# Gate matrix of an expert layer: one-hot products for 128 tokens, scattered adding transfers for the other 128

## The chip, the cores and the metric

One core of a Trainium2 chip runs the whole program: TensorE (PE in the profile; its weight loads are PEld), VectorE (DVE), ScalarE (ACT), GpSimd (POOL), SyncE (SP) and 16 DMA engines. The metric is the device time of one execution in microseconds, as the median of the runs. Less is better.

## What is computed

The reference is a transformer-like block followed by a second block, on 256 tokens of width 2048, all in float32. The part that matters here is the expert layer (PEER) of the second block: every token picks 16 experts in each of 8 heads, out of 128 x 128 experts, and gives each a gate.

```python
cand_i = (i1[..., :, None] * PEER_KEYS + i2[..., None, :]).reshape(t, PEER_HEADS, -1)
top_s, pos = lax.top_k(cand_s, PEER_TOPK)
expert = jnp.take_along_axis(cand_i, pos, axis=-1).reshape(t, -1)
gate = jax.nn.softmax(top_s.astype(jnp.float32), axis=-1).astype(x.dtype).reshape(t, -1)
...
z = jnp.einsum('cd,ced->ce', xc, u[ec])
act = jax.nn.gelu(z, approximate=False) * gc
return jnp.einsum('ce,ced->cd', act, v[ec])
```

The kernel computes it densely. For all 16384 experts it forms `z = x @ u.T`, takes the gelu, multiplies by a gate matrix G that holds the summed gate of each (expert, token) pair and is zero where the token did not pick the expert, and multiplies by `v`. G is 128 blocks of experts by 256 tokens, with 128 experts of each block on the partitions: 16.8 MB, which is the whole of the SBUF tensor `big`.

## The kernel before

**The stream.** All weights, `u` and `v` among them, arrive as 902 units of 512 KB (128 partitions x 1024 float32), two units to a pair, through four buffers `raw` that SP loads (L598). Each unit is split into a high part in float32r (`split_hi`, ACT, L474) and a low rest (`split_lo`, DVE, L483), and PE multiplies with both. A load is issued when the low half of the unit four earlier is made; ACT and DVE split units up to four ahead of PE (`w_hi`, `w_lo` have four slots each; both wait on `unit_done`). A unit is 8 matmuls of 512 columns on the high part (L540) and 8 of 256 columns on the low part (L547) in `halves_out`.

**The stages of the expert layer.** One pair of `u` gives one block of 128 experts. The 128 blocks go through three loops, then `v` is multiplied.

- `u_decode` (with `wqu`): 32 blocks while the router's picks are made.
- `u_gates`: 64 blocks, 32 turns of two pairs. Between the high and the low products of each pair, PE makes the gates of four tokens (L2558, `four_tokens`): one matmul of a one-hot of the second index (`hot`, 128x128, made by POOL at L686) with a one-hot of the first index that carries the gate's high and low half (`weighted`, 128x256, made by DVE at L2023). ACT copies the low half of the result from PSUM to G (L1160), DVE adds the high half (L2017). 64 pairs x 4 tokens = 256 tokens.
- `u_late`: 32 blocks, whose gelu is multiplied by G at once. The blocks before them could not be, since G was not there: ACT stores each to a DRAM tensor `z_kept` (128 KB a block), and `late_turn` and the first half of the `v` loop read them back into `cst` and multiply.

So the 96 early blocks make the way over DRAM, and the 32 late ones don't. The order on each engine is written out by hand; PE, ACT and DVE meet through counting semaphores. Before the gates loop the three lists of picks (first index, second index, gate; 256 tokens x 128 slots each) are transposed by PE (L2548), six matmuls of 128x128.

The kernel is built with `dynamic_dma_scratch_size=1024`, the bytes per partition that are reserved for the descriptors of POOL's transfers; before the change POOL issues none. POOL's queue in this part: staging copies of the attention (L647), sums of the router, then the 256 compares at L686, then the gain of the output at the end (L692).

Of the kernel before, what the change touches and what calls it, by code (L numbers as in the profile page):

```python
# [65 lines left out]
SLOT_N = PH * PK  # L66

# [3 lines left out]
         ("wqu", 4 * PH), ("u_decode", 2 * PH), ("u_gates", S // 4), ("u_late", NB // 4), ("v", NB)]  # L71
EARLY = 3 * NB // 4
LATE = NB - EARLY
# [11 lines left out]
for _name, _count in [("conv", 4 * CONV_J), ("rnn", 2 * KT), ("heads", 2 * H2), ("u_decode", 2 * PH), ("u_gates", S // 4),  # L85
                      ("u_late", LATE)]:
    HALVED[_name] = _n
    _n += _count
# [5 lines left out]
for _name, _count in [("ident", P), ("iota", P), ("band", TT * 2 * P), ("causal", TT * S), ("cos", TT * HALF),  # L94
                      ("sin", TT * HALF)]:
    CONST[_name] = (_n, _n + _count)
    _n += _count
# [37 lines left out]
def build(nc, stream, x, p_t, rows, consts, params, rg_w, ukv, keys_t, out):  # L135
    ctx = ExitStack()
    with ctx:
# [24 lines left out]
        with nc.sbuf_tensor("expert_act", [P, 2, 2, S], F32R) as expert_act:  # L162
            pass
        weighted = sb("weighted", [P, 4, 2, P], F32R)
# [10 lines left out]
        x_kept = nc.dram_tensor("x_kept", (P, TT * D), F32, kind="Internal").ap()  # L175
        z_kept = nc.dram_tensor("z_kept", (EARLY, P, S), F32, kind="Internal").ap()

# [98 lines left out]
        first_index = slot_t[:, 0, :]  # L276
        second_index = par[:, 0:S]
        gate_hi = slot_t[:, 1, :]
        gate_lo = slot_t[:, 2, :]
        GATE_BANKS = [[banks[0], banks[1]], [banks[4], banks[5]]]  # L280
# [31 lines left out]
        idx8 = stat[:, 8:16]  # L312
# [123 lines left out]
        hot_turn = sem("hot_turn")  # L436
        hot1 = sem("hot1")
        hot2 = sem("hot2")
# [148 lines left out]
        primed = [y_made, z_saved, early_ready, scored, rg_done, logits_made, hot2, hot_used, conv_b_used,  # L587
# [45 lines left out]
        def _(pool):  # L633
# [6 lines left out]
            pool.sem_inc(pool_summed, 4)  # L640

            for t in range(TT):
# [34 lines left out]
            pool.wait_ge(slots_kept, 3)  # L677

            with pool.Fori(0, S // 8) as i:
                pool.wait_ge(hot2, i * 8 + 1)  # L680
                pool.tensor_copy(idx8, second_index[:, bass.ds(i * 8, 8)]).then_inc(g_step, 1)
                pool.wait_ge(g_step, i + 1)
                for s in range(8):
                    pool.wait_ge(hot_used[s % 4], i * 2 + s // 4 + 1)
                    pool.sem_inc(hot_turn, 1)
                    pool.tensor_scalar(hot[:, s % 4, :], iota, idx8[:, s:s + 1], None, ALU.is_equal)\  # L686
                        .then_inc(hot2, 1)
# [9 lines left out]
        def _(act):  # L697
# [439 lines left out]
            for a in range(3):  # L1137
                act.wait_ge(picks_turned, 2 * a + 2)
                act.activation([first_index, second_index, gate_lo][a], banks[4 + a][:, 0:S], ACT.Copy).then_inc(slots_kept, 1)
# [13 lines left out]
            def gates_turn(i, first=False):  # L1153
                for n in range(2):
# [3 lines left out]
                    for half in range(2):  # L1158
                        act.wait_ge(hot_used[2 * half + 1], i * 2 + n + 2)
                        act.activation(G[:, :, bass.ds(i * 8 + (4 * n + 2 * half), 2)],  # L1160
                                       GATE_BANKS[n][half].rearrange("p (t a b) -> p a b t", t=2, a=2)[:, 1, :, :],
                                       ACT.Copy).then_inc(gate_low, 1)
# [6 lines left out]
            with act.Fori(1, S // 8) as i:  # L1169
                gates_turn(i)  # L1170
            save_gelu(S // 8 - 1, 1)
# [92 lines left out]
        def _(dve):  # L1264
# [737 lines left out]
            for a in range(3):  # L2002
                ins = dve.tensor_copy(PICKT[:, a, :, :, :].rearrange("p t h k -> p h t k"), PICK[:, a, :, :, :])
                ins.then_inc(picks_ready, 1)
# [7 lines left out]
            def add_gates(i, n):  # L2012
                for half in range(2):
                    dve.wait_ge(gate_low, i * 4 + (2 * n + half + 1))
                    dest = G[:, :, bass.ds(i * 8 + (4 * n + 2 * half), 2)]
                    high = GATE_BANKS[n][half].rearrange("p (t a b) -> p a b t", t=2, a=2)[:, 0, :, :]
                    dve.tensor_tensor(dest, dest, high, ALU.add).then_inc(gate_kept[n], 1)  # L2017

            def four_tiles(i, n):
                for s in range(4):  # L2020
                    tok = i * 8 + (4 * n + s)
                    dve.wait_ge(hot_used[s], i * 2 + n + 1)
                    dve.scalar_tensor_tensor(  # L2023
                        out=weighted[:, s, :, :], in0=iota.unsqueeze(1).broadcast_to([P, 2, P]),
# [4 lines left out]
            def gates_turn(i, last=False):  # L2029
                for n in range(2):  # L2030
                    ahead(split_lo, dve, "u_gates", i, 2, n, units=(0,))
                    if not (last and n):
                        four_tiles(i, n + 1)
# [4 lines left out]
            four_tiles(0, 0)  # L2038
            with dve.Fori(0, S // 8 - 1) as i:
                gates_turn(i)  # L2040
            gates_turn(S // 8 - 1, last=True)
            for n in range(2):
                dve.wait_ge(gate_kept[n], S // 4 + 1)
# [91 lines left out]
        def _(pe):  # L2135
# [409 lines left out]
            for a in range(3):  # L2545
                pe.wait_ge(picks_ready, a + 1)
                for t in range(TT):
                    pe.transpose(banks[4 + a][:, t * P:(t + 1) * P],  # L2548
                                 PICKT[:, a, t, :, :].rearrange("p h k -> p (h k)"),
                                 ident).then_inc(picks_turned, 1)  # L2550
            decode_turn(PH - 1)

            def four_tokens(i, n):
                pe.wait_ge(gate_kept[n], i * 2 + 1)
                pe.wait_ge(hot1, i * 8 + (4 * n + 4))
                pe.wait_ge(hot2, i * 8 + (4 * n + 4 + 1))
                for s in range(4):
                    pe.matmul(GATE_BANKS[n][s // 2][:, (s % 2) * S:(s % 2 + 1) * S], hot[:, s, :],  # L2558
                              weighted[:, s, :, :].rearrange("p a b -> p (a b)"), start=True, stop=True)\
                      .then_inc(hot_used[s], 1)  # L2560

            with pe.Fori(0, S // 8) as i:
                for n in range(2):
                    pe.wait_ge(gelu_ready[n], i + (2 * PH + 1))
                    halves_out(pe, pair_of("u_gates", i, 2, n), odd_of("u_gates", n), banks[2 + n], between=lambda: four_tokens(i, n))
# [6 lines left out]
            def expert(i, n, first=False):  # L2572
                pe.wait_ge(el_ready, i * 2 + n + 1)
                if first:
                    for m in range(2):
                        pe.wait_ge(gate_kept[m], S // 4 + 1)
# [101 lines left out]
def _constants():  # L2678
# [11 lines left out]
    return np.concatenate([np.eye(P), iota, *band, *causal, *rope], 1).astype(f)  # L2690
# [48 lines left out]
```

## Time and profile before

| | us |
|---|---|
| median of 3 runs | 2715.92 |
| lowest, highest | 2714.54, 2717.73 |
| the profiled execution | 2715.33 |
| its span, first to last instruction | 2713.5 |

Between the span and the time of the profiled execution lie 1.8 us. The granted TensorE clock is 0.999 of full over the span, so 2.4 GHz all along. The views used below are the page of the profile (busy time by engine, the chain of work that ended last, the costliest groups), stretches of the timeline, busy time by stretch, groups by line in a stretch, and the DMA queues of a stretch. An engine that is idle costs nothing where another is the bound.

### The profile page before, as it was taken

What the parts mean: (1) busy time and instruction counts of PE and PEld (TensorE: products, weight loads), DVE (VectorE), ACT (ScalarE), POOL (GpSimd) and SP (SyncE); (2) the same over time, 40 slices, a digit from 0 to 9 for tenths busy, and PEclk for the clock granted to TensorE, in tenths of its full rate; (3) what the DMA queues carried; (4) which work ended last, traced back from release to release, by engine and by line L of the source; (5) the groups of instructions that cost most, each with busy time, mean ns of one, the idle gap of its engine ahead of it and who ended that gap; (6) DMA issues with size and microseconds to landing.
All of it is one profiled execution on the core that took longest, in us unless ns stands there. A gap on an engine that the chain in (4) does not pass through costs nothing.

```text
span 2713.5 us, 48127 instructions
## 1 busy us (share of the span) xinstructions
PE 2689.9 (99%) x14366; PEld 2315.8 (85%) x14366; DVE 1879.4 (69%) x3046; ACT 1383.0 (51%) x2114; POOL 357.0 (13%) x422
## 2 busy tenths in 40 slices
PE   8999999999999999999999999999999999999998
PEld 7888888898888888888888888888888888888887
DVE  6666665658986666489897888886665555555555
ACT  6454545556655444455465555554544444444444
POOL 0000000000001110011105666660000000000000
PEclk9999999999999999999999999999999999999999
DMA  7545455555555545655566556556666666656564
GB/s 258 192 158 172 162 192 186 174 207 169 168 176 167 162 155 160 193 192 190 197 208 200 192 196 196 194 197 207 213 212 217 217 216 218 211 193 193 194 239 156
DMA packets 162488, 522.19 MB, mean 192 GB/s; under 512 B 18048, under 2 KB 42880, under 8 KB 161408
## 3 DMA queue, kind: packets, MB, share of 16 engines
q1 hardware_dynamic: 131472, 478.35, 54.4%
q10 hardware_dynamic: 30960, 43.14, 4.5%
q8 instruction: 30, 0.49, 0.1%
q14 instruction: 26, 0.21, 0.0%
HBM read 504.63 MB, written 16.78 MB: 192 GB/s over the span
## 4 chain that ended last, share of the span: by engine, by line
PE 94%; DVE 3%; ACT 1%; issue 1%; DMA 0%; SPq 0%; DVEq 0%; ACTq 0%
PE bank L540 31%; PE bank L547 16%; PE bank L2589 8%; PE bank L2591 8%; PE bank L2590 8%; PE bank L580 5%; PE bank L581 4%; PE bank L582 4%; PE bank L2558 1%; PE bank L2392 1%; PE bank L2387 1%; DVE w_lo L483 1%; PE bank L506 1%; PE bank L507 1%; PE bank L508 1%
## 5 line engine op out<-in xcount | busy, mean ns | idle before, releaser
L483 DVE TENSOR_TENSOR w_lo<-raw,w_hi 128x1024 fp32r<-128x1024 f32 x902 | 1095.6, 1224 | 690.1 <-ACT w_hi L474 683.9
L474 ACT ACTIVATE w_hi<-raw 128x1024 fp32r<-128x1024 f32 x902 | 952.2, 1060 | 937.6 <-PE bank L547 354.2
L540 PE MATMUL bank<-act,w_hi 128*128 128x512 f32 x3840 | 975.6, 396 | 2.0 <-DVE big L1433 0.8
L540 PEld LDWEIGHTS bank<-act,w_hi 128*128 128x128 f32 x3840 | 692.1, 189 | 133.1 <-issue 5.6
L547 PEld LDWEIGHTS bank<-act,w_lo 128*128 128x128 f32 x3840 | 519.9, 190 | 33.1
L547 PE MATMUL bank<-act,w_lo 128*128 128x256 f32 x3840 | 535.7, 282 | 0.0
L2589 PE MATMUL bank<-w_hi,expert_act 128*128 128x512 f32 x1008 | 392.4, 389 | 0.4 <-DVE cst L558 0.4
L2590 PE MATMUL bank<-w_lo,expert_act 128*128 128x512 f32 x1008 | 392.2, 389 | 0.0
L2591 PE MATMUL bank<-w_hi,expert_act 128*128 128x512 f32 x1008 | 392.2, 389 | 0.0
L686 POOL TENSOR_SCALAR hot<-cst,stat 128x128 fp32r<-128x128 f32 x256 | 255.1, 1010 | 129.1 <-PE bank L2558 128.8
L2589 PEld LDWEIGHTS bank<-w_hi,expert_act 128*128 128x128 f32 x1008 | 189.2, 188 | 40.0 <-DVE cst L558 0.8
L2591 PEld LDWEIGHTS bank<-w_hi,expert_act 128*128 128x128 f32 x1008 | 189.2, 188 | 39.3
L2590 PEld LDWEIGHTS bank<-w_lo,expert_act 128*128 128x128 f32 x1008 | 189.2, 188 | 39.2
L580 PE MATMUL bank<-w_hi,act 128*128 128x512 f32 x320 | 125.9, 393 | 1.9 <-DVE act L1328 1.1
L582 PE MATMUL bank<-w_hi,act 128*128 128x512 f32 x320 | 124.7, 390 | 0.0
L581 PE MATMUL bank<-w_lo,act 128*128 128x512 f32 x320 | 124.6, 390 | 0.0
L692 POOL TENSOR_TENSOR big<-big 128x1024 f32<-128x1024 f32 x2 | 5.8, 2881 | 875.2 <-DVE big L2096 875.2
L2023 DVE SCALAR_TENSOR_TENSOR weighted<-cst,slot_t 128x256 fp32r<-128x256 f32 x256 | 116.1, 511 | 0.0
L654 POOL TENSOR_TENSOR big<-big 128x256 f32<-128x256 f32 x16 | 11.2, 697 | 483.5 <-DVE big L558 483.5
L580 PEld LDWEIGHTS bank<-w_hi,act 128*128 128x128 f32 x320 | 60.1, 188 | 16.2 <-DVE act L1328 1.3
L582 PEld LDWEIGHTS bank<-w_hi,act 128*128 128x128 f32 x320 | 60.1, 188 | 12.7
L581 PEld LDWEIGHTS bank<-w_lo,act 128*128 128x128 f32 x320 | 60.1, 188 | 12.0
(330 smaller groups left out, 2462.9 us busy)
## 6 DMA issues: line engine op xcount, KB each, us to landing
raw<-in_stream SPq DMA_DIRECT2D x902, 512.0 KB, 4.1
z_kept<-cst ACTq DMA_DIRECT2D x96, 128.0 KB, 2.2
cst<-z_kept ACTq DMA_DIRECT2D x96, 128.0 KB, 3.9
big<-in_ukv ACTq DMA_DIRECT2D x16, 512.0 KB, 4.6
big<-in_rows ACTq DMA_DIRECT2D x3, 1024.0 KB, 5.6
big<-in_x SPq DMA_DIRECT2D x2, 1024.0 KB, 9.4
big<-in_rg_w ACTq DMA_DIRECT2D x1, 2048.0 KB, 9.3
x_kept<-big ACTq DMA_DIRECT2D x1, 2048.0 KB, 7.4
```

What stands on the lines that cost most here:

```text
L474: act.activation(w_hi[:, s, :], raw[:, s, :], ACT.Copy).then_inc(hi_ready, 1)
L483: dve.tensor_tensor(w_lo[:, s, :], raw[:, s, :], w_hi[:, s, :].bitcast(F32), ALU.subtract).then_inc(lo_ready, 1)
L540: pe.matmul(bank[:, :], w_hi[:, s, kk * P:(kk + 1) * P], act2[:, k, :, :].rearrange("p a n -> p (a n)"), start=(k == 0), stop=False)
L547: mm = pe.matmul(bank[:, 0:S], w_lo[:, s, kk * P:(kk + 1) * P], act_hi[:, k, :], start=False, stop=(k == KT - 1))
L580: pe.matmul(outs[t], a_hi, hi, start=(k == 0), stop=False)
L581: pe.matmul(outs[t], a_hi, lo, start=False, stop=False)
L582: mm = pe.matmul(outs[t], a_lo, hi, start=False, stop=(k == KT - 1))
L686: pool.tensor_scalar(hot[:, s % 4, :], iota, idx8[:, s:s + 1], None, ALU.is_equal)\
L2023: dve.scalar_tensor_tensor(out=weighted[:, s, :, :], in0=iota.unsqueeze(1).broadcast_to([P, 2, P]), scalar=first_index[:, bass.ds(tok, 1)] ...
L2589: pe.matmul(o, a_hi, hi, start=first, stop=False, skip_group_check=True)
L2590: pe.matmul(o, a_hi, lo, start=False, stop=False, skip_group_check=True)
L2591: mm = pe.matmul(o, a_lo, hi, start=False, stop=False, skip_group_check=True)
```

## The change

The first 128 tokens keep the one-hot products. The gates of the other 128 tokens go another way:

- **Zeroing.** A DRAM tensor `g_kept` of 128 x 128 x 128 float32 (8.4 MB, index expert * 128 + token) is filled with zeros by 16 transfers of 512 KB that POOL issues in the attention's staging loop, two after each of its 8 turns. Their source is a zeroed tile that lies where `expert_act` is later.
- **Scatter.** DVE works out the flat index (expert * 128 + partition, three small instructions in place of half the copies). POOL then issues 128 indirect transfers that add, one for each slot: 128 elements of 4 bytes, one from each partition, to 128 places of the table. Within a head's 16 slots a token has 16 different experts, so these run together; before each head POOL waits until all earlier ones have landed.
- **Read back.** After the last scatter and the last of the gated turns, POOL issues 32 transfers of 4 blocks each (128 partitions x 4 x 512 bytes = 256 KB) from the table to `G[:, b:b+4, 128:256]`. DVE waits for all of them before its first `late_turn`.
- **The gates loop.** Each pair has two tokens in place of four: two matmuls (L2588 of the changed kernel), one copy by ACT, one addition by DVE. The compares that POOL made are made by DVE (L2049). 64 pairs x 2 tokens = 128 tokens.
- **More early blocks.** After the 64 gated pairs come 16 pairs without gates; `u_late` shrinks from 32 to 16 pairs. 112 blocks, not 96, go over `z_kept`.
- Three transposes of picks in place of six.

```diff
+ZERO_DMAS = NB * P // ZERO_W
+TABLE_DMAS = 32
...
-EARLY = 3 * NB // 4
-LATE = NB - EARLY
+LATE = 2 * PH
+EARLY = NB - LATE
+GATED = P // 4
...
+                    for q in range(ZERO_DMAS // (TT * KVH)):
+                        pool.dma_start(g_zero[bass.ds(u * (ZERO_DMAS // (TT * KVH)) + q, 1), :, :]
+                                       .rearrange("o p n -> (o p) n"), zeros[:, :]).then_inc(scattered, 16)
...
-            with pool.Fori(0, S // 8) as i:
-                pool.wait_ge(hot2, i * 8 + 1)
-                pool.tensor_copy(idx8, second_index[:, bass.ds(i * 8, 8)]).then_inc(g_step, 1)
...
-                    pool.tensor_scalar(hot[:, s % 4, :], iota, idx8[:, s:s + 1], None, ALU.is_equal)\
-                        .then_inc(hot2, 1)
+            pool.wait_ge(picks_ready, 5)
+            for h in range(PH):
+
+                pool.wait_ge(scattered, 16 * (ZERO_DMAS + PK * h))
+                for i in range(h * PK, (h + 1) * PK):
+                    pool.indirect_dma_start(g_kept, bass.IndirectOffsetOnAxis(ap=SLOT_INDEX[:, i:i + 1], axis=0),
+                                            SLOT_GATE[:, i:i + 1], None, compute_op=ALU.add).then_inc(scattered, 16)
+            pool.wait_ge(scattered, 16 * (ZERO_DMAS + SLOT_N))
+            for n in range(2):
+                pool.wait_ge(gate_kept[n], GATED + 1)
+            width = NB // TABLE_DMAS
+            for q in range(TABLE_DMAS):
+                b = (q * width + EARLY) % NB
+                pool.dma_start(G[:, b:b + width, P:S], g_table[:, b:b + width, :]).then_inc(table_back, 16)
...
-            def four_tiles(i, n):
-                for s in range(4):
-                    tok = i * 8 + (4 * n + s)
-                    dve.wait_ge(hot_used[s], i * 2 + n + 1)
+            def two_tiles(i, n):
+                for s in range(2):
+                    tile = 2 * (n % 2) + s
+                    tok = i * 4 + (2 * n + s)
+                    dve.wait_ge(hot_used[tile], i + (n // 2 + 1))
+                    dve.tensor_scalar(hot[:, tile, :], iota, second_index[:, bass.ds(tok, 1)], None, ALU.is_equal)
...
+            with dve.Fori(GATED, EARLY // 2 - 2 * PH) as i:
+                for n in range(2):
+                    ahead(split_lo, dve, "u_gates", i, 2, n)
+                    add_halves(dve, GZ[:, n, :], banks[2 + n], block_of("u_gates", i, 2, n))
             for n in range(2):
-                dve.wait_ge(gate_kept[n], S // 4 + 1)
+                dve.wait_ge(gate_kept[n], GATED + 1)
+            dve.wait_ge(table_back, 16 * TABLE_DMAS)
...
-            with pe.Fori(0, S // 8) as i:
+            def two_tokens(i, n):
+                pe.wait_ge(gate_kept[n], i + 1)
+                pe.wait_ge(hot1, i * 4 + (2 * n + 2))
+                for s in range(2):
+                    pe.matmul(GATE_BANKS[n][:, s * S:(s + 1) * S], hot[:, 2 * n + s, :],
+                              weighted[:, 2 * n + s, :, :].rearrange("p a b -> p (a b)"), start=True, stop=True)\
+                      .then_inc(hot_used[2 * n + s], 1)
+
+            with pe.Fori(0, GATED) as i:
```

PE's queue in the gates loop, one of the two pairs of a turn. Before:

```order
L540 MATMUL bank<-act,w_hi 128x512 x8
L547 MATMUL bank<-act,w_lo 128x256 x8
L535 REGISTER_ALU
L540 MATMUL bank<-act,w_hi 128x512 x8
L2555 REGISTER_ALU
L2556 REGISTER_ALU
L2558 MATMUL bank<-weighted,hot 128x256 x4
L547 MATMUL bank<-act,w_lo 128x256 x8
```

The same pair in the changed kernel:

```order
L551 MATMUL bank<-act,w_hi 128x512 x8
L558 MATMUL bank<-act,w_lo 128x256 x8
L546 REGISTER_ALU
L551 MATMUL bank<-act,w_hi 128x512 x8
L2586 REGISTER_ALU
L2588 MATMUL bank<-weighted,hot 128x256 x2
L558 MATMUL bank<-act,w_lo 128x256 x8
```

Two of the four matmuls of the gates are gone from the pair, and nothing else of it moved.

POOL's queue from the last sums of the router to its end. Before:

```order
L671 COMPARE_AND_BRANCH
L679 UNCONDITIONAL_BRANCH
L679 ISA
L681 ISA
L681 COPY stat<-par 128x8
L682 REGISTER_ALU
L684 ISA
L686 ISA
L686 TENSOR_SCALAR hot<-cst,stat 128x128 x4
```

The same place in the changed kernel:

```order
L687 REGISTER_ALU
L687 COMPARE_AND_BRANCH
L698 DMA g_kept<-slot_t 2097152x1 x128
L706 DMA big<-g_kept 128x4x128 x32
L711 TENSOR_TENSOR big<-big 128x1024 x2
```

The compares are gone; the 128 scatters and behind them the 32 reads stand in their place, ahead of the output's gain.

## Rows read from the trace of the kernel before

**Rows 1.** Page: span, busy us and share by engine, DMA tenths by slice
```profile
span 2713.5 us, 48127 instructions
PE 2689.9 (99%) x14366; PEld 2315.8 (85%) x14366; DVE 1879.4 (69%) x3046; ACT 1383.0 (51%) x2114; POOL 357.0 (13%) x422
...
DMA  7545455555555545655566556556666666656564
```

**Rows 2.** Page: the chain that ended last, shares by engine
```profile
PE 94%; DVE 3%; ACT 1%; issue 1%; DMA 0%; SPq 0%; DVEq 0%; ACTq 0%
```

**Rows 3.** Timeline, gated pair: start us, length us, engine, line, operation, count
```profile
1501.78 2.00 PE L540 MATMUL bank<-act,w_hi 128*128 128x512 f32 x8
1501.98 1.06 ACT L474 ACTIVATE w_hi<-raw 128x1024 fp32r<-128x1024 f32 x1 [0.42 <-PE bank L547]
...
1503.16 1.23 DVE L483 TENSOR_TENSOR w_lo<-raw,w_hi 128x1024 fp32r<-128x1024 f32 x1 [0.31 <-ACT w_hi L474]
...
1506.41 0.64 PE L2558 MATMUL bank<-weighted,hot 128*128 128x256 f32 x4
...
1507.84 2.00 PE L540 MATMUL bank<-act,w_hi 128*128 128x512 f32 x8
```

**Rows 4.** Timeline, PE at the start of the late stretch
```profile
1829.38 2.00 PE L540 MATMUL bank<-act,w_hi 128*128 128x512 f32 x8
...
1832.17 2.00 PE L540 MATMUL bank<-act,w_hi 128*128 128x512 f32 x8
...
1834.96 2.00 PE L540 MATMUL bank<-act,w_hi 128*128 128x512 f32 x8
```

**Rows 5.** Line L2558: duration ns min/median/max, first and last start us
```profile
L2558 PE MATMUL bank<-weighted,hot x256: 277/283/380, 1445.6 to 1828.3; 128*128 128x256 f32 x128
```

**Rows 6.** Timeline, PE and ACT around the transposes of the picks
```profile
1425.73 2.00 PE L540 MATMUL bank<-act,w_hi 128*128 128x512 f32 x8
...
1428.53 0.82 PE L2548 MATMUL bank<-cst,big 128*128 128x128 f32 x6
...
1429.11 2.07 PE L540 MATMUL bank<-act,w_hi 128*128 128x512 f32 x8
...
1430.49 0.40 ACT L1139 ACTIVATE slot_t<-bank 128x256 f32<-128x256 f32 x1
```

**Rows 7.** Busy us by stretch: PE, PEld, DVE, ACT, POOL; clock, DMA share, GB/s
```profile
1446.00:1828.00 382.00, 382.00 (x2269) 339.80 (x2268) 329.14 (x568) 213.40 (x378) 257.67 (x283) 1.00 0.59 194
1842.00:1999.00 157.00, 157.00 (x900) 138.16 (x899) 100.56 (x143) 80.39 (x115) 0.00 (x0) 1.00 0.67 215
```

**Rows 8.** Groups by line, DVE, 1450 to 1820 us: busy us, mean ns
```profile
L483 DVE TENSOR_TENSOR w_lo<-raw,w_hi 128x1024 fp32r<-128x1024 f32 x122 | 149.6, 1226 | 51.5 <-ACT w_hi L474 51.5
L2023 DVE SCALAR_TENSOR_TENSOR weighted<-cst,slot_t 128x256 fp32r<-128x256 f32 x244 | 110.8, 511 | 0.0
L2017 DVE TENSOR_TENSOR big<-big,bank 128x256 f32 x122 | 48.2, 441 | 0.0
```

**Rows 9.** Groups by line, whole span: a DVE compare-like operation of 128x128
```profile
L1832 DVE TENSOR_SCALAR big<-big,stat 128x128 f32<-128x128 f32 (+1 forms) x32 | 8.8, 317 | 0.6
```

**Rows 10.** DMA queues and issues, 1500 to 1800 us: packets, MB, share; KB, us to landing
```profile
q1 hardware_dynamic: 14244, 51.86, 53.1%
q10 hardware_dynamic: 7200, 6.56, 6.3%
...
raw<-in_stream SPq DMA_DIRECT2D x99, 512.0 KB, 3.3
z_kept<-cst ACTq DMA_DIRECT2D x50, 128.0 KB, 2.1
```

**Rows 11.** DMA issues, 1830 to 2000 us
```profile
cst<-z_kept ACTq DMA_DIRECT2D x30, 128.0 KB, 4.2
```

**Rows 12.** Waits, whole span: us in total, times, longest us
```profile
POOL big L647 <- PE bank L2242: 147.6, 7, 24.5
```

More of the change, by code:

```diff
@@ L163, in build @@
             pass
+        with nc.sbuf_tensor("zeros", [P, ZERO_W], F32) as zeros:
+            pass
         weighted = sb("weighted", [P, 4, 2, P], F32R)
@@ L640, in _ @@
             pool.sem_inc(pool_summed, 4)
+            step(pool.memset(zeros[:, :], 0.0))
+            step.wait()
             for t in range(TT):
@@ L1151, in save_gelu, with gates_turn @@
                               GZ[:, n % 2, :]).then_inc(z_saved[n % 2], 16)
-            def gates_turn(i, first=False):
+            def gates_turn(i, first=False, gates=True):
                 for n in range(2):
@@ L1157, in gates_turn @@
                         save_gelu(i, n - 1)
[L1158 to L1161, printed above, removed]
+                    if gates:
+                        act.wait_ge(hot_used[2 * n + 1], i + 2)
+                        act.activation(G[:, :, bass.ds(i * 4 + 2 * n, 2)],
+                                       GATE_BANKS[n].rearrange("p (t a b) -> p a b t", t=2, a=2)[:, 1, :, :],
                                        ACT.Copy).then_inc(gate_low, 1)
@@ L1168, in _ @@
             gates_turn(0, first=True)
-            with act.Fori(1, S // 8) as i:
+            with act.Fori(1, GATED) as i:
                 gates_turn(i)
-            save_gelu(S // 8 - 1, 1)
+            with act.Fori(GATED, EARLY // 2 - 2 * PH) as i:
+                gates_turn(i, gates=False)
+            save_gelu(EARLY // 2 - 2 * PH - 1, 1)
             for n in range(2):
@@ L2002, in _ @@
             for a in range(3):
-                ins = dve.tensor_copy(PICKT[:, a, :, :, :].rearrange("p t h k -> p h t k"), PICK[:, a, :, :, :])
-                ins.then_inc(picks_ready, 1)
+                dve.tensor_copy(PICKT[:, a, 0, :, :], PICK[:, a, :, 0, :]).then_inc(picks_ready, 1)
+            step(dve.scalar_tensor_tensor(out=SLOT_EXPERT.rearrange("p (h k) -> p h k", k=PK), in0=PICK[:, 0, :, 1, :],
+                                          scalar=float(KEYS), in1=PICK[:, 1, :, 1, :], op0=ALU.mult, op1=ALU.add))
+            step.wait()
+            dve.tensor_scalar(SLOT_INDEX, SLOT_EXPERT, float(P), c("partition"), ALU.mult, ALU.add)\
+               .then_inc(picks_ready, 1)
+            dve.tensor_copy(SLOT_GATE.rearrange("p (h k) -> p h k", k=PK), PICK[:, 2, :, 1, :]).then_inc(picks_ready, 1)
             for unit in lows:
@@ L2012, in add_gates @@
             def add_gates(i, n):
[L2013 to L2017, printed above, removed]
-            def four_tiles(i, n):
-                for s in range(4):
-                    tok = i * 8 + (4 * n + s)
-                    dve.wait_ge(hot_used[s], i * 2 + n + 1)
+                dve.wait_ge(gate_low, i * 2 + (n + 1))
+                dest = G[:, :, bass.ds(i * 4 + 2 * n, 2)]
+                high = GATE_BANKS[n].rearrange("p (t a b) -> p a b t", t=2, a=2)[:, 0, :, :]
+                dve.tensor_tensor(dest, dest, high, ALU.add).then_inc(gate_kept[n], 1)
+            def two_tiles(i, n):
[4 more added lines that the diff above has]
+                    dve.tensor_scalar(hot[:, tile, :], iota, second_index[:, bass.ds(tok, 1)], None, ALU.is_equal)
                     dve.scalar_tensor_tensor(
-                        out=weighted[:, s, :, :], in0=iota.unsqueeze(1).broadcast_to([P, 2, P]),
+                        out=weighted[:, tile, :, :], in0=iota.unsqueeze(1).broadcast_to([P, 2, P]),
                         scalar=first_index[:, bass.ds(tok, 1)],
```

73 lines of the change are left out of this document (35 added, 38 removed).

## The prediction

> **What bounds the kernel now.** I read the page first. PE is busy for 2689.9 of 2713.5 us, DVE for 69%, ACT 51%, POOL 13%, and the DMA engines are at four to seven tenths in nearly every slice [rows 1]. The chain that ended last is PE for 94% [rows 2]. A busy PE is not by itself a PE at its peak, so I looked at the two stretches that the change touches: in the gates loop PE is busy for all 382 of 382 us and in the late loop for all 157 of 157, at full clock [rows 7]. No other engine is full there: in the gates loop DVE has 329 of 382 us, ACT 213, POOL 258, the DMA engines a share of 0.59. What PE no longer does there comes off the end, one for one, as long as nobody else becomes late. Nothing else that the change removes or moves is on the path.
>
> **What PE loses.** The timeline gives the period of a gated pair from two starts of the same block of L540: 1501.78 to 1507.84, 6.06 us [rows 3]. The pair without gates is in the late loop: 1829.38 to 1834.96, 5.58 us [rows 4]. The four matmuls of the gates thus cost 0.48 us, 0.12 each. Their own row says 0.64 for four [rows 3], and 283 ns for one [rows 5]; these overlap their neighbours, and I take the difference of the periods. The 64 pairs lie between 1445.6 and 1828.3 [rows 5], 63 periods of about 6.07, so the period holds all along. Two of four go: 64 x 0.24 = **15.3 us**. Three of six transposes go. The half pair that holds the six runs from 1425.73 to 1429.11, 3.38 us [rows 6], and a plain half takes 2.79 [rows 4], so six cost 0.59 and three **0.3 us**. The sixteen pairs that move from late to early cost PE the same 5.58 us. Sum: 15.6 us.
>
> **What DVE, ACT and POOL gain and lose, under PE's cover.** A pair costs DVE now two splits of 1.23, four tiles of 0.51, two additions of 0.44 and one of 0.41: 5.8 us with the gaps counted as 6.06 [rows 8]; it waits 51.5 us in 61 pairs, always for ACT's split. After the change: two splits, two tiles, one addition fewer, and two compares on DVE. The trace has no compare of 128x128 on DVE; the nearest row is a TENSOR_SCALAR of that size at 0.32 us [rows 9], and I bound it by 0 and 0.51 (the tile of twice its size). The new pair is 2.45 + 1.02 + 0.44 + 0.41 + 0.64 = 5.0 us of a period of 5.82, and 5.3 at the upper bound: covered. Without that cover each 0.1 us over the period would cost 6.4 us. ACT has one copy of 0.4 less. POOL gives up its compares altogether, and nobody waits for it in the loop but through the table. The extra 16 blocks over `z_kept` add 16 stores and 16 reads of 128 KB; the stores are beside plain pairs, the reads in the `v` loop, where the read is issued a turn ahead of its use. I cost them at nothing.
>
> **Zeroing.** 16 transfers of 512 KB in the attention, when the DMA engines are at about half [rows 1]. A 4 KB packet of the stream takes 0.531 x 16 x 300 us / (99 x 128) = 0.20 us [rows 10], so 16 x 128 packets cost each engine 26 us over a stretch of some 160 us that has about 80 free. POOL stands idle between its staging copies for 147.6 us in 7 waits, 21 us each [rows 12], so two issues per turn delay no copy. Cost 0; if they did delay one turn's copies by 2 us each, 16 us, but I see no path to that.
>
> **Where PE could be made to wait: the table.** DVE waits for all 32 reads before its first late turn, and behind that wait stand the splits of all later units, and so SP's loads and PE. What is the window? POOL starts the reads when DVE has added the last gates. DVE then has 16 plain pairs, 16 x 5.58 = 89 us. A late DVE is not at once a late PE: ACT's split starts at 1501.98, when PE has finished a unit, the low part is ready at 1504.39 [rows 3], and PE comes to it three units and eight matmuls later, 3 x 2.79 + 1.84 = 10.2 us after the start. DVE may be late by 7.8 us; I count 7, since SP's next load hangs on it too. Window: **96 us** from the first issue to the last landing. Landing of the last one takes 2 to 4 us [rows 10, 11], so the 32 have to follow each other at 2.9 us or less. At 3.4 us each (stall 15.6) the gain is eaten. Two things set that pace.
>
> (a) The DMA engines. In the gates loop stream and stores hold a share of 0.594 [rows 10] of 6.06 us; in a plain pair that is 0.594 x 6.06 / 5.58 = 0.645, free 0.355. The table is 16384 rows of 512 bytes, 1024 per engine. A 1 KB packet of the stores takes 0.063 x 16 x 300 us / (50 x 128) = 47 ns [rows 10]. Half the size is between half of that and all of it: 24 to 48 us per engine. At a share of 0.355 the first needs 68 us; of the second 34 us are done in the window and 14 remain: a stall of 0 to 14. Since 4 KB take 0.20 us and 1 KB 47 ns, the time so far goes with the bytes, and I take the value near 24 to 30 us: no stall.
>
> (b) POOL's issue, of which this trace has no row: POOL issues no transfer. Bounds: a hardware-queue issue with its landing at 2.1 us [rows 10] for 128 KB, and 4.2 us beside the stream [rows 11]. If each had to land before the next, 32 would take 67 to 134 us: a stall of 0 to 38. I take the lower part, because several can be under way: nothing in the code waits between them.
>
> The Trainium skill, "DMA: Bandwidth & Descriptors", section "Anatomy of one DMA — SWDGE (gpsimd) path", gives a transfer issued by GpSimd about 2.0 us plus its bytes at 436 GB/s. By that page a table read of 262,144 bytes is an estimated 2.6 us, 32 in a row 83 us, and the sum would have no stall even without overlap.
>
> **The scatter.** It may start when the picks are ready, near 1430 [rows 6], and must be over when the gated turns end, 1446 + 64 x 5.82 = 1818: 388 us for 128 transfers, 3.0 us each. They move 64 KB in all. Nearest rows: again 2.1 to 4.2 us from issue to landing. At 2.1 one by one 269 us, hidden; at 4.2, 538. Sixteen at a time may be under way, so I take hidden. Their load on the engines: 1024 small packets each; at 47 ns 48 us over 388, a share of 0.12 on top of 0.62. The stream's loads land in 3.3 us and are needed about 6 us later than that (four units of 2.8 to 3.3 us, less two splits and the landing), so they bear it.
>
> **Sum.** 2715.3 (the profiled execution, 0.6 below the median) - 15.3 - 0.3 = **2699.7 us**.
>
> **Rivals.**
>
> *Partly hidden.* The 512-byte rows cost an engine nearly what 1 KB costs, or the scatter's packets hold the stream up a little. Stall 2 to 14 us: 2702 to 2714. For it: the free share is only 0.355. Against: cost has gone with bytes so far.
>
> *The table comes late (slower).* The kernel reserves 1024 bytes per partition for the descriptors of POOL's queue, and a table read has 32 rows per engine. If POOL has room for barely one read at a time, or needs more than 3.4 us to write one with its 512 rows, DVE stands at its wait, and PE a little later. At 4.2 us each [rows 11], 32 x 4.2 = 134 against 96: stall 38, **2738 us**. It decides from 3.4 to 3.5 us per read on; every 0.5 us more costs 16. For it: a load of the stream has 8 rows per engine, this read has 32, with half the bytes. Against: a stream unit of twice the bytes lands in 3.3 us [rows 10].
>
> The same page, section "SWDGE vs HWDGE vs iDMA", says that a GpSimd core writes these descriptors in software into a ring in SBUF, 16 bytes each by its section "Terms"; no row here shows it.
>
> *The scatter comes late.* At over 3.0 us per scatter the reads start late. At 4.2 it ends 150 us late: about 2850.
>
> *The change doesn't relieve PE.* DVE would have to pass 5.82 us per pair; it has 5.0. Under 1 in 50.
>
> **Chances.** Hidden 0.52, partly hidden 0.17, table late 0.22, scatter late 0.07, the rest 0.02. A measurement of this kernel tells 0.2% from no change, 5.4 us. Faster by more than that means under 2710.5, a stall under 10: hidden and two thirds of partly hidden, 0.62. Within 0.2% (stall of 10 to 21): the rest of it and the mild end of the late table, 0.11. Slower: 0.27. Range for 8 in 10: from 2697 (0.12 us per matmul may be 0.14) to 2745, which takes in the late table at 4.2 us per read and leaves out the worse of it and the late scatter.
>
> **What would show it.** Period of a gated pair near 5.82 us and 5.58 in the 16 plain pairs; no idle PE between them and the `v` loop; DVE's wait before its first late turn short; the scatters over before about 1818 us. Wrong if the reads' last landing is more than 96 us behind the last gated addition: then PE shows one gap of that length at the start of the late loop. Wrong in size if L2588's pair of matmuls costs other than 0.24 us. If the stream is disturbed, ACT's splits wait for `raw` in the scatter's stretch.

## The result, and the profile after

| | before | after |
|---|---|---|
| median, us | 2715.64 | 2769.2 |
| lowest, highest of 4 runs | 2714.54, 2717.73 | 2768.13, 2772.15 |
| span of the profiled execution | 2713.5 | 2770.4 |

The ratio is 1.0198, with a 95% interval from 1.0185 to 1.021: **54 us slower**. Forecast were 2699.7 us, with a range up to 2745. The profiled execution is the slowest of the four (2772.15). The page of the changed kernel:

```profile
span 2770.4 us, 46922 instructions
PE 2677.4 (97%) x14235; PEld 2302.6 (83%) x14235; DVE 1820.0 (66%) x2985; ACT 1363.0 (49%) x2050; POOL 370.2 (13%) x311
...
PEclk9999999999999999999999999998699999999999
DMA  6566555555555445655677777775366666666664
...
q0 software_dynamic: 23296, 16.85, 3.7%
...
PE 75%; issue 11%; POOL 9%; DVE 2%; DMA 2%; ACT 1%; SPq 0%; ACTq 0%; DVEq 0%
```

Against [rows 1] PE is 12.5 us less busy, yet the span is 57 us longer. The chain of [rows 2] was PE for 94%; now POOL has 9% of it and "issue" 11%, POOL's idle time between its transfers. In one place the granted clock drops and the DMA engines have little to do. PE's timeline there (start us, length us):

```profile
1912.90 2.00 PE L551 MATMUL bank<-act,w_hi 128*128 128x512 f32 x8
1914.75 1.11 PE L558 MATMUL bank<-act,w_lo 128*128 128x256 f32 x8
1985.43 3.77 PE L551 MATMUL bank<-act,w_hi 128*128 128x512 f32 x8 [69.57 <-DVE cst L569]
1989.00 1.60 PE L558 MATMUL bank<-act,w_lo 128*128 128x256 f32 x8
1990.44 1.99 PE L551 MATMUL bank<-act,w_hi 128*128 128x512 f32 x8
```

PE stands still for 69.6 us. It resumes at half clock: eight matmuls take 3.77 us in place of 2.00 and the next eight 1.60 in place of 1.11, some 2.3 us more. At the end of the stall the granted clock is that of the lower level, 0.50, which is 1.2 GHz (columns: stretch, PE, PEld, DVE, ACT, POOL busy, clock, DMA share, GB/s; the stretch 1910 to 1982 still holds 6 us of PE's work):

```profile
1860.00:1908.00 48.00, 48.00 (x275) 42.18 (x275) 23.80 (x26) 23.33 (x35) 7.05 (x10) 1.00 0.80 259
...
1910.00:1982.00 72.00, 5.86 (x35) 4.98 (x33) 0.00 (x0) 2.27 (x3) 15.05 (x20) 0.56 0.27 81
1982.00:1984.00 2.00, 0.00 (x0) 0.00 (x0) 1.40 (x2) 0.00 (x0) 0.00 (x0) 0.50 0.00 0
```

The difference adds up: 69.6 + 2.3 - 15.6 (the forecast gain) = 56.3, and the spans differ by 56.9. So nearly the whole result is one stall, less the gain.

Its cause stands in the waits of DVE, and in POOL's two lines (duration ns min/median/max, first and last start us):

```profile
DVE w_lo L494 <- DMA big<-g_kept: 75.1, 1, 75.1
```

```profile
L698 POOL DMA_INDIRECT g_kept<-slot_t x128: 1554/1577/2603, 1419.9 to 1844.6; - x128
```

```profile
L706 POOL DMA_DIRECT2D big<-g_kept x32: 747/752/830, 1850.1 to 1978.9; - x32
...
DMA to landing us min/median/max: 3.0/3.2/6.0
```

The scatters run from 1419.9 to 1847, 3.3 us each, where 3.0 was the limit: the reads start at 1850 in place of 1818. They take 129 us to the last issue, 4.2 us each, where 2.9 was the limit. POOL itself is busy for 1.9 us of a scatter's 3.3 (the mean; the median is 1.6) and 0.75 of a read's 4.2. How it spends the rest is seen in its timeline:

```profile
1840.40 1.55 POOL L698 DMA_INDIRECT g_kept<-slot_t  x1 [2.83 <-issue]
1842.26 2.06 POOL L698 DMA_INDIRECT g_kept<-slot_t  x1 [0.30 <-issue]
1844.62 2.49 POOL L698 DMA_INDIRECT g_kept<-slot_t  x1 [0.30 <-issue]
1850.07 0.83 POOL L706 DMA_DIRECT2D big<-g_kept  x1 [2.96 <-DMA g_kept<-slot_t]
1853.59 0.79 POOL L706 DMA_DIRECT2D big<-g_kept  x1 [2.69 <-issue]
1859.53 0.75 POOL L706 DMA_DIRECT2D big<-g_kept  x1 [5.16 <-issue]
```

Scatters come in groups of up to three, 0.30 us apart, and then nothing for some 2.9 us. Reads come singly, with 2.6 to 5.6 us between them. No semaphore wait stands there in the code. The gaps look like POOL waiting for what it has issued, and for the reads the trace settles it, since it holds the landing of each: every one of the 31 later reads starts 0.30 us after the landing of the one before it. The read issued at 1913.12 lands 3.3 us later, at 1916.4, and the next starts at 1916.70. Why POOL waits is what the experiments test, with three theories.

**Theory R (room).** The kernel reserves 1024 bytes per partition for the descriptors of POOL's transfers. Suppose that this is room for 64 descriptors per DMA engine, 16 bytes each. A read of 4 blocks has 32 rows per engine; with one descriptor for the completion it would take 33. Then a second does not fit, and POOL waits until the first has landed. **Theory F (fixed cost):** any POOL transfer costs 3 to 4 us. **Theory S (share):** the DMA engines beside the stream are the limit.

### The profile page after: what moved, and what is told of

Same layout as the page of the kernel before. It is cut to its first block, busy times and chain, and to the rows that moved or that the text cites. A ratio compares the mean times of both kernels' runs of the same rounds, so it can differ in the third digit from the quotient of the medians.

```text
span 2770.4 us, 46922 instructions
## 1 busy us (share of the span) xinstructions
PE 2677.4 (97%) x14235; PEld 2302.6 (83%) x14235; DVE 1820.0 (66%) x2985; ACT 1363.0 (49%) x2050; POOL 370.2 (13%) x311
## 4 chain that ended last, share of the span: by engine, by line
PE 75%; issue 11%; POOL 9%; DVE 2%; DMA 2%; ACT 1%; SPq 0%; ACTq 0%; DVEq 0%
PE bank L551 20%; PE bank L558 10%; PE bank L2623 8%; PE bank L2624 8%; PE bank L2625 8%; POOL g_kept L698 8%; PE bank L591 4%; PE bank L593 4%; PE bank L592 4%; DMA g_kept<-slot_t 1%; PE bank L2425 1%; PE bank L2420 1%; POOL big L706 1%; DVE w_lo L494 1%; PE bank L517 1%
## 5 line engine op out<-in xcount | busy, mean ns | idle before, releaser
L698 POOL DMA_INDIRECT g_kept<-slot_t x128 | 238.9, 1866 | 254.4 <-issue 171.3
L670 POOL TENSOR_TENSOR big<-big 128x256 f32<-128x256 f32 x16 | 11.1, 696 | 482.5 <-DVE big L569 482.5
L685 POOL TENSOR_TENSOR big<-big 128x256 f32<-128x256 f32 x32 | 33.1, 1033 | 248.1 <-ACT big L1087 248.1
```

The source lines that it names most:

```text
L685: pool.tensor_tensor(dest, halves[:, 0:S], halves[:, S:2 * S], ALU.add).then_inc(pool_summed, 1)
L698: pool.indirect_dma_start(g_kept, bass.IndirectOffsetOnAxis(ap=SLOT_INDEX[:, i:i + 1], axis=0), SLOT_GATE[:, i:i + 1], None, compute_op=AL ...
```

## The experiments

### Without the reads: is it only the table?

```diff
-            for q in range(TABLE_DMAS):
-                b = (q * width + EARLY) % NB
-                pool.dma_start(G[:, b:b + width, P:S], g_table[:, b:b + width, :]).then_inc(table_back, 16)
+            pool.memset(G[:, :, P:S], 0.0).then_inc(table_back, 1)
```

> The changed kernel with its 32 table reads left out: POOL fills the second half of G with zeros in one memory operation in their place (so the gates of tokens 128 to 255 are left out of the output). The zeroing and the 128 scatters stay. Theory: the 57 us of the change are a stall of 69.6 us before the late loop, 2.3 us at half clock after it, less 15.6 us of PE work; without the reads nothing comes late, since the scatters end at 1846 us and DVE needs the table only near 1908. So 2700 us, a ratio of 0.994 to before, gated pairs at 5.82 us. Rival (the scatters' small packets or DVE's compares also cost PE time): 2703 to 2715, with gaps on PE between 1446 and 1814 us.

Measured: 2700.01 us, ratio 0.9941 [0.9925, 0.9958]. All of the loss hangs on the reads and their lateness, and the scatters beside the stream cost PE nothing: it is busy for all 360 of 360 us between 1450 and 1810, here and in the changed kernel. The gain is the forecast one, and the changed kernel's own timeline of PE shows it:

```profile
1500.50 2.00 PE L551 MATMUL bank<-act,w_hi 128*128 128x512 f32 x8
...
1505.13 0.40 PE L2588 MATMUL bank<-weighted,hot 128*128 128x256 f32 x2
...
1506.33 2.00 PE L551 MATMUL bank<-act,w_hi 128*128 128x512 f32 x8
```

The period is 5.83 us; [rows 3] had 6.06.

### Without the scatters: do the two delays add?

```diff
-                for i in range(h * PK, (h + 1) * PK):
-                    pool.indirect_dma_start(g_kept, bass.IndirectOffsetOnAxis(ap=SLOT_INDEX[:, i:i + 1], axis=0),
-                                            SLOT_GATE[:, i:i + 1], None, compute_op=ALU.add).then_inc(scattered, 16)
```

> The changed kernel without the 128 scatters (the table stays zero, so the gates of tokens 128 to 255 are left out of the output); the 32 reads stay as they are. The reads can then start when the gated turns end, near 1818 us instead of 1850. Theory (two delays that add): the stall falls from 69.6 by 32 to about 38 us, total 2737 to 2740. Rival (the reads are slow because the scatters have clogged the queue): reads at under 3 us each and no stall, 2700. Rival (the scatters' lateness is all of it): 2700 as well.

Measured: 2750.13 us, ratio 1.0127 [1.011, 1.0144]. PE's stall is 49.8 us:

```profile
PE bank L551 <- DVE cst L569: 49.8, 1, 49.8
```

The reads alone are too slow, so neither rival holds. The two delays add, though not one for one: the reads started 33 us earlier, at 1816.6, and the stall fell by 20. Reads beside the stream are the slow ones: POOL waits 2.9 to 6.2 us after them and 2.6 to 2.9 us in the stall. Here 19 of the 32 are issued before the stall, in the changed kernel 13 were. The first reads:

```profile
1816.63 0.82 POOL L703 DMA_DIRECT2D big<-g_kept  x1 [465.08 <-DVE big L2039]
1820.94 0.77 POOL L703 DMA_DIRECT2D big<-g_kept  x1 [3.50 <-issue]
1827.83 0.75 POOL L703 DMA_DIRECT2D big<-g_kept  x1 [6.12 <-issue]
1832.08 0.76 POOL L703 DMA_DIRECT2D big<-g_kept  x1 [3.50 <-issue]
```

I had taken the same pace in both places. Six reads more at 5.1 us in place of 3.5 make an estimated 10 of my 12 us of miss.

### Twice as many reads of half the size

```diff
-TABLE_DMAS = 32
+TABLE_DMAS = 64
```

> The changed kernel with 64 reads of 128 KB (2 blocks) in place of 32 of 256 KB; same bytes, same rows of 512 bytes. Theory R (room): POOL's queue has 1024 bytes per partition for descriptors, and a read of 4 blocks takes more than half of it, so only one is under way and each waits for the one before it to land. With half the size three fit, they overlap, and all 64 take 70 to 90 us in place of 132: 2705 to 2735 us. Theory F (fixed cost): each read costs its 3.4 to 4.2 us whatever its size: 64 take 218 to 269 us, total 2855 to 2910. Theory S (the DMA engines' share is what limits): no change, 2769.

Measured: 2754.73 us (2749.7 to 2766.7), ratio 1.0135 [1.0118, 1.0152]. Theory F is out by more than 100 us: twice the transfers are not slower but 14 us faster. POOL's timeline shows the groups of three that theory R wanted (17 descriptors each, 51 of 64), beside the stream in the first two rows and in the stall in the last two:

```profile
1872.35 2.13 POOL L706 DMA_DIRECT2D big<-g_kept  x3 [4.85 <-issue]
1878.91 2.12 POOL L706 DMA_DIRECT2D big<-g_kept  x3 [4.42 <-issue]
...
1921.25 2.13 POOL L706 DMA_DIRECT2D big<-g_kept  x3 [2.27 <-issue]
1925.57 2.13 POOL L706 DMA_DIRECT2D big<-g_kept  x3 [2.19 <-issue]
```

My size for it was wrong, 70 to 90 us for the reads where they took 112. I had assumed that a fourth read follows as soon as the first of the three has landed. Instead POOL writes three and waits for the last of them. Of the group that starts at 1872.35 the first read lands at 1876.3 and the last at 1878.6, and the next group starts at 1878.91. In all 21 cases POOL goes on 0.34 to 0.35 us after the landing of a group's last read. For the reads, then, the queue is not kept full; it is filled and emptied. A group of three halves carries 1.5 times the bytes of a whole read, and that is the gain. In the profiled run, the slowest of the four, the scatters also ended 15 us later than in the changed kernel (last start 1860.1), which hides part of it.

### More room: 2560 bytes, and 1536

```diff
-        slot_t = sb("slot_t", [P, 3, S])
+        slot_t = sb("slot_t", [P, 3, P])
...
-        SLOT_INDEX = slot_t[:, 0, P:S].bitcast(U32)
-        SLOT_GATE = slot_t[:, 1, P:S]
+        SLOT_INDEX = par[:, P:2 * P].bitcast(U32)
+        SLOT_GATE = par[:, 2 * P:3 * P]
...
-    nc = bacc.Bacc("TRN2", target_bir_lowering=False, num_devices=1, dynamic_dma_scratch_size=1024)
+    nc = bacc.Bacc("TRN2", target_bir_lowering=False, num_devices=1, dynamic_dma_scratch_size=2560)
```

> The changed kernel with 2560 bytes per partition reserved for the descriptors of POOL's transfers in place of 1024; to make the space, the scatter's indices and gates lie in an SBUF tensor that is no longer in use. Nothing else changes. Theory R (room): the scatters follow each other at POOL's own 1.6 to 2.2 us plus 0.3, so the last ends near 1710 us in place of 1846; the reads start at 1818 and follow each other at 1 to 2 us, 35 to 65 us in all; no stall, 2700 us. Theory F (fixed cost of a POOL transfer) and theory S (the DMA engines' share): no change, 2769.

Measured: **2699.84 us**, ratio 0.9941 [0.9924, 0.9958]. One number of the build takes 69 us off the changed kernel (the control below shows that the moved lists do not), and it is now 16 us faster than the kernel before. POOL's scatters and reads:

```profile
1426.19 1.60 POOL L698 DMA_INDIRECT g_kept<-par  x1 [0.30 <-issue]
...
1437.73 1.56 POOL L698 DMA_INDIRECT g_kept<-par  x1 [0.30 <-issue]
1442.78 1.55 POOL L698 DMA_INDIRECT g_kept<-par  x1 [3.48 <-issue]
...
1468.47 1.78 POOL L698 DMA_INDIRECT g_kept<-par  x1 [4.06 <-issue]
...
1484.06 1.56 POOL L698 DMA_INDIRECT g_kept<-par  x1 [0.30 <-issue]
...
1816.87 3.12 POOL L706 DMA_DIRECT2D big<-g_kept  x4 [49.47 <-DVE big L2042]
1827.09 3.00 POOL L706 DMA_DIRECT2D big<-g_kept  x4 [7.10 <-issue]
```

There are eight scatters in a row (from 1424.32 to 1437.73), three times nine (the first from 1468.47 to 1484.06), and four reads in a row each time (4 x 33 = 132 of 160; five would be 165). POOL again goes on 0.35 us after a group's last landing: the first read lands at 1820.8, the fourth at 1826.7, the fifth is issued at 1827.09. The reads' waits remain, but there are 7 in place of 31. The scatters' last start is 1764.9, 55 us later than I expected, since their waits remain too, 28 in place of 58; the last read is issued at 1884.6 and lands at 1890.9. What the DMA engines do meanwhile is the answer to theory S (columns: stretch, PE, PEld, DVE, ACT, POOL busy, clock, DMA share, GB/s):

```profile
1821.00:1888.00 67.00, 67.00 (x386) 58.97 (x385) 33.33 (x37) 32.37 (x48) 20.86 (x28) 1.00 0.94 323
```

They carry 323 GB/s at a share of 0.94, stream included, and PE is busy for 67 of 67 us. In the changed kernel they had 0.80 and 259 GB/s beside the stream, and 0.27 around the stall, where a read still took 3.5 us. So the share was there to be had.

With 1536 bytes (96 descriptors), the same edit otherwise:

> As the run with 2560 bytes of descriptor space, but with 1536 bytes, so 96 descriptors of 16 bytes per engine in place of 64 (the changed kernel) or 160. Theory R, as the runs so far show it: POOL writes transfers until the next one doesn't fit, then waits until those have landed. A read of 4 blocks takes 33: one at a time in 64, four in 160. In 96 two should fit, and a scatter, at about 18 each, five. So reads come in pairs, one pair each 6.5 to 7 us beside the stream, 105 to 112 us in all; the last scatter near 1790 to 1815; a stall of 10 to 20 us: 2710 to 2722 us. Theory F (no such room) would leave singles at 4.2 us: 2750 to 2769.

Measured: 2711.85 us (10 runs, 2708.5 to 2715.8), ratio 0.9985 [0.9976, 0.9995]; reads in pairs, as 2 x 33 fit:

```profile
1826.30 1.50 POOL L706 DMA_DIRECT2D big<-g_kept  x2 [5.60 <-issue]
1831.87 1.50 POOL L706 DMA_DIRECT2D big<-g_kept  x2 [4.07 <-issue]
...
1925.17 3.77 PE L551 MATMUL bank<-act,w_hi 128*128 128x512 f32 x8 [9.26 <-DVE cst L569]
```

A stall of 9.3 us, and the half clock after it again. The three sizes make a series: 64, 96 and 160 descriptors, reads in ones, twos and fours, stalls of 69.6, 9.3 and 0 us.

The lists of indices and gates had to move to make the space. A control with 1024 bytes and the moved lists:

> Control for the runs with more descriptor space: the changed kernel with its 1024 bytes, but with the scatter's indices and gates in the tensor that those runs put them in. Theory R: the place of the lists means nothing, 2765 to 2770 us, reads one at a time. If the place were what helped, 2700.

Measured in two runs: 2770.94 us (2764.4 and 2777.5), ratio 1.0203 [1.0174, 1.0231], reads one at a time. Their place takes nothing off the time.

### Scatters that write in place of adding

```diff
-                                            SLOT_GATE[:, i:i + 1], None, compute_op=ALU.add).then_inc(scattered, 16)
+                                            SLOT_GATE[:, i:i + 1], None).then_inc(scattered, 16)
```

> The changed kernel (1024 bytes of descriptor space) with scatters that write instead of adding, so where two heads of a token pick the same expert only the last gate is kept in the output. Theory R with two descriptors on one side for each added element (the old value and the new one are both read): an adding scatter takes 17 or 18 descriptors per engine, three fit; a plain one takes 9 and seven fit. So runs of seven with 0.3 us between them, the last scatter before 1760 us; the reads then start at 1817 as in the run without scatters: 2750 us. If adding costs the queue no room, the scatters keep their groups of one to three, end near 1840, and the time is 2765 to 2770.

Measured: 2750.13 us (two runs), ratio 1.0126 [1.0106, 1.0146], the time of the run without scatters.

```profile
L698 POOL DMA_INDIRECT g_kept<-slot_t x128: 962/972/2013, 1418.6 to 1655.8; - x128
...
L706 POOL DMA_DIRECT2D big<-g_kept x32: 747/752/803, 1817.9 to 1957.7; - x32
```

A plain scatter costs POOL 0.97 us, an adding one 1.58, and the 128 are over after 237 us in place of 425. The longest run in a group is seven (1429.30 to 1437.41), where the adding ones have three. With 8 elements and a completion per engine, nine descriptors, seven fit in 64. The longest groups of adding ones are three in 64, five in 96 and nine in 160. If theory R holds for them, only 17 descriptors each fit all three: at 16, four would fit in 64, and at 18 no nine in 160. 17 is twice 8 elements and a completion. That an added element needs two descriptors is argued from these counts and not seen.

Two things stay open. Most groups of adding scatters are shorter than the longest: in the changed kernel 26 groups have three, 17 two and 16 one. And at the start of each later head POOL has waited until everything has landed, yet it issues only one or two scatters before the next gap, though an empty queue would hold three. So for scatters the room alone does not give the counts, and the trace holds no landings of theirs.

The adding also costs the DMA engines time. Between 1450 and 1600 us the changed kernel's 46 scatters made 6480 packets and held the 16 engines at 12.6%; 81 plain ones made 2544 packets at 1.2%. Neither cost PE time.

### Other ways round: a later deadline, another queue

A split wait, with 1024 bytes. The late loop needs only 8 of the 32 reads:

```diff
-                pool.dma_start(G[:, b:b + width, P:S], g_table[:, b:b + width, :]).then_inc(table_back, 16)
+                pool.dma_start(G[:, b:b + width, P:S], g_table[:, b:b + width, :])\
+                    .then_inc(table_back if q < first_reads else scattered, 16)
...
-            dve.wait_ge(table_back, 16 * TABLE_DMAS)
+            first_reads = 2 * LATE * TABLE_DMAS // NB
+            dve.wait_ge(table_back, 16 * first_reads)
...
+            dve.wait_ge(scattered, 16 * (ZERO_DMAS + SLOT_N + TABLE_DMAS - first_reads))
             with dve.Fori(0, (EARLY - LATE) // 2) as i:
```

> The changed kernel, 1024 bytes of descriptor space, but DVE waits before the late loop only for the first 8 of the 32 reads (blocks 112 to 127 and 0 to 15, all that the late loop uses), and for the other 24 before the loop over v. Theory (the stall is the lateness of the reads against a deadline, nothing else): 8 reads end near 1850 + 8 x 4.9 = 1889, before 1908; the other 24 near 2008, and the loop over v needs them near 1999 + 7. So a stall of 0 to 10 us, 2700 to 2710. Rival (reads beside the stream hurt the stream): waits of ACT for the stream's units, 2715 or more.

Measured: 2716.87 us (10 runs, 2705.9 to 2726.8), ratio 1.0000 [0.9985, 1.0014]. It gives back 52 us, but not all, the runs spread over 21 us, and the median lies above the expected 2710, in the range of the rival. The profiled run (2708.7 us of span, one of the faster ones) decides: the last read is issued at 2006.9, DVE waits 13.0 us for it, and PE stops for 8.5 us at the start of the loop over v. No wait of ACT for `raw` stands in that stretch, so the rival, a disturbed stream, shows nothing there. Why the runs spread is not shown, as only one has a trace. A likely cause is the end of the scatters: in five traces of other kernels with the same scatters and 1024 bytes, the last one starts anywhere between 1834.5 and 1869.1, and here the reads end right at the deadline.

With more room and the split together nothing is near its deadline:

> 1536 bytes of descriptor space together with the split wait (8 reads before the late loop, 24 before the loop over v). In 1536 bytes the last of 32 reads was issued at 1918 us, 9 us of PE too late; the split moves its deadline by 89 us. No stall on PE: 2700 us, and runs that agree within 3 us, since nothing is near its deadline.

Measured: 2700.23 us (2699.8 to 2701.9), ratio 0.9944 [0.9927, 0.996].

> 2560 bytes of descriptor space together with the split wait. With 2560 bytes alone the reads were over some 20 us before they were needed, so more room before the deadline gives nothing: 2700 us, as without the split (2699.8).

Measured: 2699.52 us (2698.8 to 2699.8), ratio 0.9940 [0.9923, 0.9956]. As expected, this is no faster than 2560 bytes alone; no table read is late any more.

Reads from ACT's queue, 1024 bytes:

```diff
+            act.wait_ge(table_free, 32)
+            for n in range(2):
+                act.wait_ge(gate_kept[n], GATED + 1)
+            width = NB // TABLE_DMAS
+            for k in range(4):
+                for q in range(8 * k, 8 * k + 8):
+                    b = (q * width + EARLY) % NB
+                    act.dma_start(G[:, b:b + width, P:S], g_table[:, b:b + width, :]).then_inc(table_back, 16)
+                gates_turn(GATED + 4 + k, gates=False)
```

> The changed kernel, 1024 bytes of descriptor space, with the 32 reads issued by ACT (8 before each of the last four turns of the gates loop) in place of POOL. The scatters stay with POOL and end near 1846 us. Theory R (POOL's descriptor room is the limit, not the DMA engines): ACT's queue has no such limit, the reads need 30 to 50 us from 1863 on and are over before 1915: 2700 us, or up to 2705 if ACT's eight issues in a row (0.35 us each) make one of its splits late. Theory S (the DMA engines' share): the reads would end as late as before, 2750 to 2769.

Measured: 2719.77 us (10 runs, 2716.8 to 2731.1), ratio 1.0017 [1.0008, 1.0027]. It lies between the two theories' times, so the total decides nothing; the trace does, which is that of the slowest run (2731.1). The line of the reads and three of the four longer stops of PE:

```profile
L1195 ACTq DMA_DIRECT2D big<-g_kept x32: 397/531/2844, 1872.1 to 1922.3; - x32
...
1879.29 3.77 PE L552 MATMUL bank<-act,w_hi 128*128 128x512 f32 x8 [13.30 <-ACT cst L1163]
1895.81 2.10 PE L552 MATMUL bank<-act,w_hi 128*128 128x512 f32 x8 [2.74 <-ACT cst L1163]
...
1926.32 3.78 PE L552 MATMUL bank<-act,w_hi 128*128 128x512 f32 x8 [5.21 <-ACT cst L1163]
```

The reads' issues span 50 us in place of 129, in four batches with one turn's work (two pairs) between: theory R's side. But an issue takes ACT 0.4 to 2.8 us, not 0.35, and eight of them 5.6 to 9 us, in which ACT splits nothing. And ACT stood waiting for the scatters, which ended at 1871 in this execution: that wait and the first eight issues (1872.1 to 1877.7) make the longest stop, 13.3 us. PE now waits for ACT, 24 us in four stops, as the waits have it. The experiment put a new cost in place of the old one; fewer issues at a time were not tried.

## Why the prediction was wrong, point by point

**PE's gain: right.** Two matmuls of a pair at 0.12 us each, a gated period of 5.82 (measured 5.83), 15.6 us in all: the four kernels in which nothing comes late have 2700.0, 2699.8, 2700.2 and 2699.5, against 2699.7.

**DVE, ACT, the extra early blocks, the zeroing: right.** DVE's compares take 0.32 us, the value of [rows 9]; DVE is busy for 267 of 360 us of the gates loop (1450 to 1810) and waits for ACT, as before. That is 4.3 us of a pair, where I had added up 5.0: the durations of the single operations overlap, so my sums for DVE, 5.8 us before and 5.0 after, were too high, on the safe side. The zeroing raised the DMA share of its stretch (141 to 301 us) from 0.50 to 0.62. PE was busy there for 159.3 of 160 us, against all 160 before: at most 0.7 us, where I had 0.

**The window: right.** 96 us from the first issue to the last landing. Without scatters the first issue was at 1816.6 (forecast 1818) and the last landing at 1960.0, 143.4 us later. By the window that gives a stall of 47.4 us, and 49.8 were measured.

**The pace that the DMA engines allow, (a): right.** 1024 rows of 512 bytes per engine were put at 24 to 30 us of each. In the stall of the changed kernel 19 reads took 25.4% of 65 us, 16.5 us, so 32 take 28.

**POOL's issue, (b): the step that failed.** It was bounded at 67 to 134 us, the upper end being one read landed before the next is issued, and I took the lower part "because several can be under way: nothing in the code waits between them". The code doesn't wait, but POOL does: with 1024 bytes each read is issued only after the one before has landed, 4.2 us per read where 2.9 was the limit. The measured 132 us are near the upper bound by luck: 13 reads went at 5.1 us and 19 at 3.5 in the stall that they made. Without the scatters it was 143 us, over the bound. That 64 descriptors hold one read of 33 I could have reckoned from the build line and the shape of the read: it stood in the rival, as "room for barely one read at a time", but without the count, and against it I held a landing of 3.3 us on SP's queue. That row tells nothing of POOL's queue.

The Trainium skill, "DMA: Bandwidth & Descriptors", section "Anatomy of one DMA — SWDGE (gpsimd) path", has a fixed 2.0 us and the bytes at 436 GB/s, by which a read is an estimated 2.6 us. The trace does not agree: a read alone in the queue took 3.5 us from issue to issue in the stall and 5.1 beside the stream.

**The scatter: failed in the same way.** 3.0 us each was the limit, I took "sixteen at a time", and it was one to three at a time and 3.3 us each. That an adding scatter costs POOL 1.6 times the time of a plain one, and comes in groups of three at most where plain ones come in sevens, was in no row. Its load on the DMA engines was right: a share of 0.12, as forecast.

**The rivals.** Both late rivals came true at once. The late table was priced at 2738, 4.2 us per read; alone it measured 2750.1 us, 4.5 us per read, which is already above the upper end of 2745. The late scatter, 3.3 us each in place of 3.0, started the reads 33 us later and added the other 19 us. That 2738 and 32 also make 2770 is luck. I had given the two 0.22 and 0.07 and never priced them together, though both depend on how many transfers POOL can have under way.

**The clock.** The 2.3 us at 1.2 GHz after the stall stood in no term.

## What to carry to other kernels

Before you hide transfers that GpSimd issues, divide the bytes reserved for its descriptors by 16 and by the rows per engine plus one (for an adding scatter twice its elements per engine, plus one): the result, rounded down, is the most that were under way here, and each group of reads cost a full landing. Give the queue more room first; where there is none, smaller transfers that fill the room better can be faster than large ones, here by 14 us. Take the landing from a place as busy as yours: 3.5 us in the stall was 5.1 beside the stream. And price two risks that share a cause together: here the reads alone cost 50 us and the late scatters 19 more.

## What the runs showed of the hardware

- For plain reads POOL's queue is filled and emptied, not kept full: the next group starts 0.30 to 0.36 us after the last landing of the one before, in all 74 cases of four kernels. After a read of 256 KB POOL stays idle for 2.6 to 2.9 us in the stall and for 2.7 to 6.2 beside the stream, after three of 128 KB for 2.1 to 2.4 and 3.9 to 5.3, and after four of 256 KB beside the stream for 5.2 to 7.3.
- GpSimd needs 0.75 us for a read of 512 rows and 0.71 us for one of 256, so hardly anything for the rows; 0.97 us for a plain scatter of 128 elements, 1.58 for an adding one (medians). By the packets between 1450 and 1600 us an adding one makes 141 of them and a plain one 31.
- With 2560 bytes the 16 DMA engines ran at 0.94 and 323 GB/s for 67 us, and the stream's loads landed in 5.1 us in place of 3.3 [rows 10], without a stop of PE: the four buffers covered that.
- After stops of 5.2, 9.3 and 13.3 us PE resumed at 1.2 GHz just as after the one of 69.6: the first eight matmuls took 3.77 or 3.78 us each time. After stops of 1.3 and 2.7 us they took 2.10.
